# Mixer gates of a two-layer encoder step: from plain tiles to nine seven-product units a layer

## What is computed

```python
proj = u @ w_in                      # u: 640 x 1024; the last 3 x 1024 columns are gate logits gl
y_pool, y_att, y_conv = ...          # 256, 512 and 256 wide
gates = sigmoid(gl + b_gate)         # three gates (branches), each 640 x 1024
merged = (gates[0] * (y_pool @ w_branch[:256])
          + gates[1] * (y_att @ w_branch[256:768])
          + gates[2] * (y_conv @ w_branch[768:]))
m = merged @ w_out;   h = h + rmsnorm(m)
```

## Time and profile before

| | us |
|---|---|
| median of 3 runs | 2654.51 (2653.41 to 2654.93) |
| the profiled execution | 2655.74 |
| its span, first to last instruction | 2653.9 |
| PE busy | 2632.4 (99%) |
| DVE busy | 1705.1 (64%) |
| ACT busy | 1073.1 (40%) |
| POOL busy | 901.3 (34%) |
| granted TensorE clock, mean | 0.998 of full |

### The profile page before, as it was taken

The page is one execution under the profiler, slowest core; times in us unless marked ns, Lnnn a source line. Parts: engine busy times, 40 slices in busy tenths (PEclk is TensorE's granted clock), DMA queues, the critical chain, the costliest instruction groups (busy, mean ns, idle before and its releaser), DMA issues.

```text
span 2653.9 us, 52846 instructions
## 1 busy us (share of the span) xinstructions
PE 2632.4 (99%) x17936; PEld 2592.2 (98%) x17936; DVE 1705.1 (64%) x2592; ACT 1073.1 (40%) x1938; POOL 901.3 (34%) x730
## 2 busy tenths in 40 slices
PE   9999999999999999999999999999999999999998
PEld 8999999989999999999999999998999999999998
DVE  7888824664454888882488886266554457988623
ACT  5444513333333544452344444143333344444412
POOL 4655203140001565530256651043100035666112
PEclk9999999999999999999999999999999999999999
DMA  4232323212222222323222232231222222322321
GB/s 131 72 93 81 88 77 90 85 48 73 78 74 82 62 73 81 92 75 87 84 72 80 79 94 85 69 109 54 65 71 71 81 79 58 87 79 87 88 73 62
DMA packets 431022, 210.44 MB, mean 79 GB/s; under 512 B 44777, under 2 KB 429259, under 8 KB 430859
## 3 DMA queue, kind: packets, MB, share of 16 engines
q1 hardware_dynamic: 427252, 205.17, 27.0%
q10 hardware_dynamic: 3638, 3.51, 0.4%
HBM read 205.12 MB, written 5.29 MB: 79 GB/s over the span
## 4 chain that ended last, share of the span: by engine, by line
PE 92%; DVE 6%; ACT 1%; issue 1%; POOL 1%; DVEq 0%; ACTq 0%; POOLq 0%
PE ps L755 11%; PE ps L757 11%; PE ps L756 11%; PE ps L661 9%; PE ps L663 9%; PE ps L662 9%; PE ps L860 7%; PE ps L861 7%; PE ps L862 7%; PE ps L691 5%; PE ps L743 4%; DVE mid_lo L2022 2%; PE ps L1010 1%; PE ps L988 1%; PE ps L891 1%
## 5 line engine op out<-in xcount | busy, mean ns | idle before, releaser
L2447 POOL TENSOR_TENSOR w_lo<-raw,w_hi 128x512 fp32r<-128x512 f32 x288 | 426.5, 1491 | 362.9 <-ACT w_hi L1193 361.2
L755 PE MATMUL ps<-x_r,w_hi 128*128 128x320 f32 x1728 | 534.2, 309 | 0.0
L757 PE MATMUL ps<-x_r,w_lo 128*128 128x320 f32 x1728 | 534.0, 309 | 0.0
L1761 DVE TENSOR_TENSOR w_lo<-raw,w_hi 128x1024 fp32r<-128x1024 f32 (+1 forms) x236 | 289.8, 1232 | 340.7 <-ACT w_hi L1201 340.6
L2398 POOL TENSOR_TENSOR acc_y<-acc_y,sq 128x320 f32<-128x320 f32 x95 | 95.3, 1003 | 1086.8 <-ACT sq L1211 1083.4
L756 PE MATMUL ps<-x_r,w_hi 128*128 128x320 f32 x1440 | 445.0, 309 | 0.0
L1201 ACT ACTIVATE w_hi<-raw 128x1024 fp32r<-128x1024 f32 (+1 forms) x244 | 248.9, 1026 | 470.7 <-PE ps L862 293.9
L860 PE MATMUL ps<-mid_hi,w_hi 128*128 128x320 f32 x1392 | 433.6, 311 | 5.1 <-DVE mid_lo L2022 4.5
L861 PE MATMUL ps<-mid_lo,w_hi 128*128 128x320 f32 x1392 | 430.2, 309 | 0.0
L862 PE MATMUL ps<-mid_hi,w_lo 128*128 128x320 f32 x1392 | 430.1, 309 | 0.0
L661 PE MATMUL ps<-x_r,w_hi 128*128 128x320 f32 x1088 | 345.3, 317 | 0.0
(11 more groups left out here) (235 smaller groups left out, 5093.0 us busy)
## 6 DMA issues: line engine op xcount, KB each, us to landing
raw<-in_ffn_w_gate_dram SPq DMA_DIRECT2D x352, 128.0 KB, 2.3
raw<-in_ffn_w_up_dram SPq DMA_DIRECT2D x352, 128.0 KB, 2.3
raw<-in_ffn_w_down_dram SPq DMA_DIRECT2D x348, 128.0 KB, 2.2
raw<-in_w_in_dram SPq DMA_DIRECT2D x304, 128.0 KB, 2.3
raw<-in_w_branch_dram SPq DMA_DIRECT2D x64, 128.0 KB, 2.6
raw<-in_w_out_dram SPq DMA_DIRECT2D x64, 128.0 KB, 2.3
raw<-in_ffn_w_down_dram SPq DMA_DIRECT2D x68, 64.0 KB, 1.9
rows<-in_x_prompt_dram SPq DMA_DIRECT2D x4, 512.0 KB, 6.0
```

The costliest lines, as they stand in the source:

```text
L755: pe.matmul(bank(b), wh, lhs(0, k), start=begin and k == 0, stop=False, skip_group_check=True)
L757: mm = pe.matmul(bank(b), wl, lhs(0, k), start=False, stop=k == QK - 1, skip_group_check=True)
L1761: dve.tensor_tensor(w_cols(1, hi_slot, 0, nk), raw_cols(raw_slot, 0, nk), f32(w_cols(0, hi_slot, 0, nk)), ALU.subtract).then_inc(w_split, 1)
L2447: pool.tensor_tensor(w_cols(1, slot, k0, k0 + QK), src, f32(w_cols(0, slot, k0, k0 + QK)), ALU.subtract).then_inc(ws_lo, 1)
```

## The change

In each layer tiles 0 and 1 keep the plain form, now written out instead of looped. Tiles 2 to 7 are taken two at a time; for each pair and each of the three branches there is one seven-product unit, nine units u = 0 to 8, branch u % 3 (b0, b1, b2). The product order of a unit on PE is P1, P2, P6, P5, the branch products of the previous unit's second tile, P7, P4, P3, the branch products of its own first tile. Branch rows no longer ride in a weight pair: SP brings them tile by tile into `br_raw`, ACT splits them in `branch_high`, DVE in `branch_low`, into a free part of slot 3. They have three banks of their own. The x sums are made during tiles 0 and 1 (`block_sums` on DVE, `sums_high` on ACT, lows on POOL). Weight sums, splits, snapshots and quarters C11, C12, C21, C22 have orders written out for every engine. The merged tiles lie in a buffer `mg`, and their split goes to x_r; the first w_out pair takes depth tiles 0 to 5 first. The 18 state stores move from after the loop to after the loads of unit 1, and ACT and DVE wait for them before the units.

The diff, cut to its core (indentation reduced):

```diff
+PLAIN_M = 2
+GATE_U = 3 * (KD - PLAIN_M) // 2
+PLAIN_PAIRS = MIX_PROJ + 2 * PLAIN_M
...
+BRANCH_K = ((0, 2), (2, 6), (6, 8))
+BRANCH_BANKS = (4, 6, 7)
+QUARTERS = (("C11", 0, 0), ("C21", 0, 1), ("C12", 1, 0), ("C22", 1, 1))
...
+def gate_unit(u):
+    for s in range(2):
+        slot = 2 * ((PLAIN_PAIRS + u) % 2) + s
+        free = (w_split, w0 + 2 * (PLAIN_PAIRS + u) + s - 3) if u < 2 else (gu_lo, low_gate("B22", l, u - 2))
+        load(slot, columns(w_in, l, 0, KD, COL_GATE + D * (u % 3) + P * gate_tile(u, s), slot), free)
...
+for u in range(2):
+    gate_unit(u)
 sp.wait_ge(pc_made, l + 1)
...
+for u in range(GATE_U):
+    if u + 2 < GATE_U:
+        gate_unit(u + 2)
+    else:
+        out_pair(u + 2 - GATE_U, [(gu_lo, low_gate("B22", l, u))] * 2)
+    for s in range(2):
+        branch(u, s)
+for i in range(2, KD // 2):
+    out_pair(i)
 last = w0 + MIX_TILES
-head(1, l, [(w_split, last - 1), (w_split, last), (w_split, last - 3), (w_split, last - 2)])
...
+a, z = BRANCH_K[u % 3]
+pe.wait_ge(br_split, branch_no(l, u, s))
+for hf in range(2):
+    r = 4 * u + 2 * s + hf
+    if r >= 3:
+        pe.wait_ge(br_out, 4 * GATE_U * l + r - 2)
+    b = BRANCH_BANKS[r % 3]
+    for k in range(a, z):
+        wh, wl = (w_tile(part, 3, QK + branch_at(u, s)[0] + k - a) for part in range(2))
+        pe.matmul(bank(b), wh, br_op(0, k, hf), start=k == a, stop=False)
+        pe.matmul(bank(b), wh, br_op(1, k, hf), start=False, stop=False)
+        mm = pe.matmul(bank(b), wl, br_op(0, k, hf), start=False, stop=k == z - 1)
+    mm.then_inc(br_done, 1)
...
+for u in range(GATE_U):
+    at, a, d = GATE_U * l + u, BANK_A[u % 2], BANK_D[u % 2]
+    first = u == 0
+    pe.wait_ge(gu_w0_lo, at + 1)
+    if u >= 2:
+        pe.wait_ge(gu_c21_out, at - 1)
+    else:
+        pe.wait_ge(evac, g_end + (4 if u else 1))
+    product("P1", u, lambda part, k: x_op(part, k, 0), a, True)
+    if not first:
+        pe.wait_ge(gu_c11_out, at)
+    product("P2", u, lambda part, k: x_op(part, QK + k, 0), BANK_E, True)
+    pe.wait_ge(gu_lo, low_gate("T2", l, u))
+    pe.wait_ge(gu_snap1, at + 1)
+    product("P6", u, lambda part, k: s_op(1, part, k), a, False, made(1) if first else None)
+    pe.wait_ge(gu_lo, low_gate("T1", l, u))
+    if u >= 2:
+        pe.wait_ge(gu_c12_out, at - 1)
+    else:
+        pe.wait_ge(evac, g_end + 4)
+    product("P5", u, lambda part, k: s_op(0, part, k), d, True, made(0) if first else None)
+    if not first:
+        branch(u - 1, 1)
+    pe.wait_ge(gu_lo, low_gate("T3", l, u))
+    pe.wait_ge(gu_snap2, at + 1)
+    product("P7", u, lambda part, k: x_op(part, k, 1), a, False, s3_made if first else None)
+    pe.wait_ge(gu_lo, low_gate("T4", l, u))
+    pe.wait_ge(gu_snap3, at + 1)
+    product("P4", u, lambda part, k: x_op(part, QK + k, 1), a, False)
+    pe.wait_ge(gu_lo, low_gate("B22", l, u))
+    pe.wait_ge(gu_c22_out, at + 1)
+    product("P3", u, lambda part, k: s_op(2, part, k), d, False, made(2) if first else None)
+    branch(u, 0)
+branch(GATE_U - 1, 1)
...
-with pe.Fori(0, KD) as m:
+for m in range(PLAIN_M):
     pm, gm = m * 2 + MIX_PROJ, g + 4 * MIX_PROJ + 12 * m
...
-        pe.wait_ge(mg_ready, 2 * KD * l + 2 * KD - 1 + q // 2)
-    group(tile_of(po, q % 2), q % 2, go + q, q, mg_op, K8, q // 2)
-pair_groups(po + 1, po + 1, go + 4, mg_op)
+gates(l, g + 4 * MIX_PROJ + 12 * PLAIN_M)
+po, go = PLAIN_PAIRS, g + 4 * MIX_PROJ + 12 * PLAIN_M
+pe.wait_ge(gu_c21_out, GATE_U * (l + 1))
+pe.wait_ge(gu_c12_out, GATE_U * (l + 1))
+for ks in (range(6), range(6, KD)):
+    for q in range(4):
+        pe.wait_ge(w_split, tile_of(po, q % 2))
+        for k in ks:
+            pe.wait_ge(mg_ready, 2 * KD * l + MG_ORDER.index((k, q // 2)) + 1)
...
+def branch_high(u, s):
+    act.wait_ge(br_in[s], branch_in(l, u, s))
+    copy(branch_cols(0, u, s), branch_raw(u, s)).then_inc(br_hi_made, 1)
...
+w0_high(0)
+for what in ("T1", "T2", "T4"):
+    t_high(what, 0, None)
+b22_high(0)
+for k in range(QK):
+    difference_high(k)
+for u in range(GATE_U):
+    at, a = GATE_U * l + u, BANK_A[u % 2]
+    final = u == GATE_U - 1
+    if u:
+        sigmoid(u - 1, "C12", gu_scaled, scaled_no(u - 1, 3))
+    snap(u, "P1", s1[u % 2][:, :], a, (gu_c11_out, at - 1) if u >= 2 else None, gu_snap1)
+    sigmoid(u, "C11", gu_scaled, scaled_no(u, 1))
+    if u:
+        branch_high(u - 1, 1)
+    snap(u, "P6", u2[u % 2][:, :], a, (gu_c12_out, at - 1) if u >= 2 else None, gu_snap2)
+    if final:
+        merged_high(range(0, 2))
+        pair_high(PLAIN_PAIRS, 0, None)
+        merged_high(range(2, 4))
+        products("P5", u)
+        pair_high(PLAIN_PAIRS, 1, None)
+        merged_high(range(4, 6))
+    else:
+        w0_high(u + 1)
+        t_high("T1", u + 1, "P5")
+        t_high("T2", u + 1, "P6")
+    snap(u, "P7", u3[:, :], a, (gu_c22_out, at) if u else None, gu_snap3)
+    if not final:
+        t_high("T3", u + 1, "P7")
+    sigmoid(u, "C22", gu_scaled, scaled_no(u, 2))
+    if final:
+        merged_high(range(6, 8))
+        branch_high(u, 0)
+        branch_high(u, 1)
+        merged_high(range(8, 10))
+        products("P4", u)
+        merged_high(range(10, 12))
+    else:
+        t_high("T4", u + 1, "P4")
+        branch_high(u, 0)
+    sigmoid(u, "C21", gu_c21_out, at + 1)
+    if not final:
+        b22_high(u + 1)
+sigmoid(GATE_U - 1, "C12", gu_scaled, scaled_no(GATE_U - 1, 3))
+merged_high(range(12, 16))
...
+    act.wait_ge(gs_d3, QK * l + k + 1)
+    act.wait_ge(group_done, g + 4 * MIX_PROJ + 12 * PLAIN_M)
     alone(act)
-    copy(at_tile(mg_hi, m, hf), xv[hf][:, :]).then_inc(mg_hi_made, 1)
-def merge_tile(m, last):
-    gm, u = g + 4 * MIX_PROJ + 12 * m, 6 * KD * l + 6 * m
+    act.activation(x_op(0, k, 1), (acc_x + acc_y)[k][:, :], ACT.Copy, scale=gcol(l, 2, k)).then_inc(gs3_hi, 1)
+def sums_high(k):
+    at = QK * l + k
+    if k:
+        act.wait_ge(gs_made, 3 * at - 2)
+    act.activation(sq[0][:, :], tile(h, QK + k, 1), ACT.Copy, scale=gcol(l, 2, QK + k)).then_inc(gs_a22, 1)
+    for j in range(3):
+        act.wait_ge(gs_made, 3 * at + j + 1)
+        copy(s_op(j, 0, k), (sq[1], diag[0], diag[1])[j][:, :]).then_inc(gs_hi, 1)
...
+def gate_sums_second(l, u):
+    r0, r1 = raw_gate(u, 0), raw_gate(u, 1)
+    made = 4 * (GATE_U * l + u)
+    dve.wait_ge(gu_w0_lo, GATE_U * l + u + 1)
+    dve.wait_ge(gu_t_made, made + 1)
+    dve.tensor_tensor(raw_cols(r0, 0, QK), t_one[:, :], raw_cols(r1, QK, KD), ALU.subtract).then_inc(gu_t_made, 1)
+    dve.wait_ge(gu_t_made, made + 3)
+    dve.tensor_tensor(raw_cols(r0, QK, KD), raw_cols(r0, QK, KD), raw_cols(r0, 0, QK), ALU.add).then_inc(gu_t_made, 1)
...
+def branch_low(u, s):
+    dve.wait_ge(br_hi_made, branch_no(l, u, s))
+    dve.tensor_tensor(branch_cols(1, u, s), branch_raw(u, s), f32(branch_cols(0, u, s)),
+                      ALU.subtract).then_inc(br_split, 1)
...
+for u in range(GATE_U):
+    at, final = GATE_U * l + u, u == GATE_U - 1
+    if u:
+        quarter12(u - 1)
+        scale12(u - 1)
+        merges(u - 1, 0)
+    if not final:
+        gate_sums_first(l, u + 1)
+    products("P2", u)
+    dve.wait_ge(gu_snap1, at + 1)
+    dve.tensor_tensor(gate_at(u, "C11"), bank(BANK_E), s1[u % 2][:, :], ALU.add).then_inc(gu_c11_out, 1)
+    scale_own(u, "C11", 0, (gu_c11_out, at + 1))
+    if u:
+        branch_low(u - 1, 1)
+    if final:
+        merged_low(range(0, 2))
+        pair_low(PLAIN_PAIRS, 0)
+        merged_low(range(2, 4))
+    else:
+        gate_w0_low(l, u + 1)
+        gate_sums_second(l, u + 1)
+    if u:
+        merges(u - 1, 1)
+    if final:
+        pair_low(PLAIN_PAIRS, 1)
+        merged_low(range(4, 6))
+    dve.wait_ge(gu_snap3, at + 1)
+    dve.tensor_tensor(gate_at(u, "C22"), bank(BANK_D[u % 2]), u3[:, :], ALU.add).then_inc(gu_c22_out, 1)
+    scale_own(u, "C22", 1, (gu_c22_out, at + 1))
+    if final:
+        merged_low(range(6, 8))
+        branch_low(u, 0)
+        branch_low(u, 1)
...
-with dve.Fori(0, KD) as m:
-    own_.loop(m, 2)
-    pm, gm, u = m * 2 + MIX_PROJ, g + 4 * MIX_PROJ + 12 * m, 6 * KD * l + 6 * m
+def block_sums(k):
...
+    at = QK * l + k
+    s1_, s2_, s4_ = sq[1][:, :], diag[0][:, :], diag[1][:, :]
+    dve.wait_ge(gs_lo, 3 * at)
+    dve.wait_ge(gs_a22, at + 1)
+    dve.scalar_tensor_tensor(out=s1_, in0=tile(h, k, 1), scalar=gcol(l, 2, k), in1=sq[0][:, :],
+                             op0=ALU.mult, op1=ALU.add).then_inc(gs_made, 1)
+    dve.wait_ge(gs_made, 3 * at + 1)
+    dve.scalar_tensor_tensor(out=s2_, in0=tile(h, k, 0), scalar=gcol(l, 2, k), in1=s1_,
+                             op0=ALU.mult, op1=ALU.subtract).then_inc(gs_made, 1)
+    dve.wait_ge(gs_made, 3 * at + 2)
+    dve.scalar_tensor_tensor(out=s4_, in0=tile(h, QK + k, 0), scalar=gcol(l, 2, QK + k), in1=s2_,
+                             op0=ALU.mult, op1=ALU.add).then_inc(gs_made, 1)
+for m in range(PLAIN_M):
+    p, gm, u = MIX_PROJ + 2 * m, g + 4 * MIX_PROJ + 12 * m, 6 * PLAIN_M * l + 6 * m
     gate(0, u, gm, 0)
     gate(1, u, gm + 1, 1)
```

(36 more changed lines are left out.)

304 lines of the change are left out of this document (261 added, 43 removed).

## The result

The changed kernel takes 2694.3 us in the median (2692.8 to 2694.6) against 2654.0 (2653.4 to 2654.9): a ratio of 1.0150, 95% interval 1.0133 to 1.0168, slower by 40 us. The direction is the one forecast and the time lies in the range, but the size is twice the 20 us that the sum gave.

A forecast was written before the change was run, and what follows sets the result against it. PE, busy 99% of the span, was taken as the bound. Terms: -31.7 + 14.0 + 16.8 + 17 + 4 = +20.1 us, giving a median of 2675 us, slower; 8-in-10 range 2643 to 2706.

The forecast's parts named there:

- matmuls removed: Gate units: 12 fewer matmuls in each of 18 units, 216 at 0.1467 us, 31.7 us less in all.
- wait 1: P4 must wait until ACT has copied P7's bank: about 0.8 us in each of 18 units, 14.0 us.
- wait 2: After P3, branch(u,0) waits for DVE's low half, held by POOL: 1.2 us in 14 units, 16.8 us (3 to 34).
- entry, waits: From plain tile 1 through unit 0, PE waits for other engines: 8.5 us per layer, 17 in all (8 to 28).
- entry, clock: Clock expected at 1.00; a rival had short waits halving it in the units, about 100 us on top, chance 0.03.
- rest: P3 waiting for C22 in a few units and unit 8's branch wait: 4 us together (0 to 10); tail nothing.

The follow-up runs named there:

- e_yield: Changed kernel, with GpSimd's low half of the next unit's T4 waiting until VectorE has finished branch(u,0)'s low half; 2680.0 us, ratio 1.0098 to before.
- e_order: Changed kernel, with branch(u,0)'s high half ahead of T4's on ScalarE and its low half ahead of C21 on VectorE; 2676.1 us, ratio 1.0080 to before.
- e_filler: Changed kernel, with TensorE doing unread extra products in front of P1, P6, P7 and P4 of unit 0; 2692.7 us, ratio 1.0143 to before.
- e_move: Changed kernel, with P7 ahead of the previous unit's second branch product and C22 ahead of the second merges on VectorE; 2682.8 us, ratio 1.0107 to before.
- e_entry: Changed kernel, with ScalarE reordered around unit 0 only: T3 and w0 highs and the copies of P1, P6, P7 earlier; 2689.1 us, ratio 1.0131 to before.
- e_all: Changed kernel, joining P7 moved forward, branch rows staged early, entry order on all queues, tail slots and P7's copy ahead of T2; 2667.5 us, ratio 1.0051 to before.

## Why the prediction was right in sign and half in size

Per layer, us of PE time lost in layer 0, against the terms of the sum:

| term | forecast | measured |
|---|---|---|
| matmuls removed | -15.8 | -15.8 |
| wait 1, P7 to P4 | 7.0 (9 units) | 6.2 (units 1 to 8) |
| wait 2, branch(u,0), units 1 to 7 | 8.4 | 7.8 |
| entry, waits | 8.5 | 10.5 with unit 0's wait 1 |
| entry, clock | 0 | 3.4 |
| rest: C22, unit 8, tail | 2.0 | 2.4 + 0.6 + 0.9 + 1.8 |
| remainder, in pieces under 0.25, the longer first matmuls among them | 0 | 1.4 |
| sum | 10.1 | 19.2 |

- **Wait 1** came out nearly as worked: 0.78 in each unit up to P4's first start (0.20 until ACT starts, 0.44 for the copy, 0.14 until PE starts), and 0.07 more within that matmul, 0.85 against the 0.8 of the forecast. The restart of 0.06 had been read behind a DVE operation and holds there (738.27 to 738.33); behind ACT's copy it is 0.14. The chain through one bank has no slack and cost the same 16 times.
- **Wait 2** came out at 1.12 on average against 1.2, through the mechanism named: e_yield took POOL away and e_order took the queue away, and each removed about what it should (14.3 and 18.2 us; expected were 13.6 and, with unit 0, 16.5 and the longer first matmuls).
- **The entry's waits** were placed right. Before unit 0, 3.5 to 4 were forecast and 3.75 lost, but 1.43 of it at the plain merge, which was put at 0.6 to 1.0; P6 1.2 to 2.6 and 2.16; P7 1, and 0.70 in layer 0, 2.26 in layer 1, where the clock had not yet fallen. Low for layer 0 was the copy of P7: 1.6 beyond wait 1, measured 2.3, and 1.6 in layer 1; the DVE sum before T2 was itself held by POOL (1.63 in place of 0.69). The stores ran from 644.05 to 650.20, as forecast, and held nobody.
- **The clock** is the first step that failed. The text gave a fall 0.03, as a matter of the steady units, and expected 1.00 everywhere. It fell in the entries. I had read only one idle of 1.1 us, though the trace of before holds a fall at 911 us, and asked nothing of pieces of 2 to 3 us close together, though the forecast itself had put them there. Its net price was small (e_filler: 1.6 us in two layers by the medians, 3.1 by the traces), but in the account it lies on top.
- **The rest** is the second: 2 forecast, 5.8 measured. "0 to 0.8" for C22 overlooked that `merges` has two additions with two SBUF inputs, both held (2.44 in place of 0.88), though the rule for that stood in the same text. The w_out pair's two passes were called free because their 72 matmuls cover the splits; nobody asked when the slots that the next pair needs come free.

What the e_move, e_entry and e_all runs add: the losses are not a plain sum. Under each of the named chains lay another, shorter by 0.2 to 3 us. A list of waits prices only the last of them.

Open stays what a separate buffer for the branch rows would give: I found no free place of that size in the layout, and it was not tried. The single slow stretch of 10.2 us in layer 1 is one execution's: e_move, e_yield and e_order, which leave the entry as it is, have two of 3.4 us there, as in layer 0, with 0.7 lost at P7 and 3.1 at P4. Why it came once as one piece the runs don't tell.

## What to carry to other kernels

When a change trades matmuls for work on the other engines, write out for each new wait what stands ahead of the releaser in its queue, and then what would be last if that were gone; a removed stall is worth only the distance to the next chain. A pass split in two moves the time at which its buffers come free, so look at the next stage's loads as well. An arithmetic saving of 1.2% turned into a loss of 1.5%; putting each queue in the order in which TensorE wants its operands brought back 49.5 of the 72 us between the two, without one operation less.

## What the runs showed of the hardware

- A DVE operation with two SBUF inputs that meets a POOL split ends about when POOL does, 0.2 to 0.55 us behind it: 128x256 subtraction 0.43 alone, 1.29 beside POOL; two 128x320 additions 0.88 and 2.44; 128x512 sum 0.69 and 1.67. Operations with a PSUM input kept 0.48 (731.27 and 738.20, both beside POOL).
- The granted clock fell to half behind idle pieces of 2 to 3 us in an otherwise busy PE, and with those filled by products that nobody reads it stayed at 1.00; units with two or three waits of 0.6 to 1.3 us each kept 1.00. At 911 us of the kernel before it fell behind waits of 0.53 and 0.66.
- A PE wait of 0.62 us in the list costs 0.85: 0.78 between the starts of matmuls, as the record before it is 0.31 long and the spacing 0.15, and 0.07 within the first matmul (0.38 in place of 0.31; 0.42 behind DVE's low part). PE starts 0.06 after DVE's low part ends and 0.14 after ACT's copy does.
- In the entry half clock cost little: with full clock P1, P6, P7 and P4 of unit 0 started within 0.12 us of the same times.
